# Which expert units the two one-use buffers hold: the second expert's, or the last group's first two

## The reference

```python
logits = (hf @ w_router).astype(jnp.float32) + b_router.astype(jnp.float32)
top_logit, top_e = lax.top_k(logits, TOP_K)          # 4 of 32 experts per token
gate = jax.nn.softmax(top_logit, axis=-1)
...
def expert_block(args):
    xb, e = args
    glu = xb @ w_gate[e] + b_gate[e]
    lin = xb @ w_up[e] + b_up[e]
    return clamped_swiglu(glu, lin) @ w_down[e] + b_down[e]
...
ys = lax.map(expert_block, (xs, block_e)).reshape(L, D).astype(jnp.float32) * row_gate[:, None]
out = jnp.zeros((M + 1, D), jnp.float32).at[row_tok].add(ys)[:M]
...
return rms_norm(h, final_norm_g)
```

## Time and profile before

| | |
|---|---|
| three runs, device time | 1239.42, 3041.05, 4169.03 us (median 3041.05) |
| span of the profiled execution | 1234.6 us |
| that execution's own device time | not given apart from its span; the lowest run is 4.8 us above the span |
| PE busy | 1154.9 us (94%) |
| DVE, ACT, POOL busy | 411.2, 261.5, 20.5 us |
| DMA moved | 458.40 MB, 371 GB/s over the span |
| chain that ended last | PE 64%, DMA 29%, SP's queue 3% |

### The profile page before, as it was taken

How to read it: one execution, slowest core, us unless ns; L and a number is a source line. 1 busy time by engine, 2 the same in 40 slices (tenths; PEclk the granted TensorE clock), 3 DMA queues, 4 the chain that set the end, 5 groups by cost and what they waited for, 6 DMA issues and landing times.

```text
span 1234.6 us, 16160 instructions
## 1 busy us (share of the span) xinstructions
PE 1154.9 (94%) x6694; PEld 577.1 (47%) x6694; DVE 411.2 (33%) x803; ACT 261.5 (21%) x451; POOL 20.5 (2%) x40
## 2 busy tenths in 40 slices
PE   9999999999999999999899897999988899989896
PEld 8888989887433333332233232433332333324331
DVE  5788573765421222221122112212221122122112
ACT  6556464364400010010001000100100010001001
POOL 3000000000000000000000000000000000000000
PEclk9999999999999999999999999999999999999999
DMA  7655424986799999999999999999999999999996
GB/s 285 225 200 196 180 97 186 379 319 245 273 405 416 427 421 434 431 429 434 430 435 428 433 432 429 430 429 433 431 429 434 432 432 431 429 434 431 421 415 270
DMA packets 30694, 458.40 MB, mean 371 GB/s; under 512 B 3648, under 2 KB 3664, under 8 KB 9904
## 3 DMA queue, kind: packets, MB, share of 16 engines
q1 hardware_dynamic: 29232, 454.05, 88.2%
q0 software_dynamic: 832, 2.51, 0.6%
q10 hardware_dynamic: 576, 1.07, 0.2%
HBM read 456.57 MB, written 1.05 MB: 371 GB/s over the span
## 4 chain that ended last, share of the span: by engine, by line
PE 64%; DMA 29%; SPq 3%; ACT 2%; issue 1%; DVE 1%; ACTq 0%; DVEq 0%
PE bank L1938 22%; DMA ring<-in_w_down 16%; DMA ring<-in_w_gate_up 12%; PE bank L1960 11%; PE bank L1507 5%; PE bank L1484 4%; PE sums L1594 3%; PE sums L1484 3%; PE sums L1507 3%; SPq L435 3%; PE sums L1889 3%; PE bank L1879 2%; PE bank L1594 2%; PE bank L1951 2%; PE sums L1533 1%
## 5 line engine op out<-in xcount | busy, mean ns | idle before, releaser
L1938 PE MATMUL bank<-ring,reg_a 128*64 128x512 f32 x2016 | 459.2, 607 | 39.0 <-DMA ring<-in_w_gate_up 38.2
L1938 PEld LDWEIGHTS bank<-ring,reg_a 128*64 128x64 f32 x2016 | 142.5, 139 | 322.0 <-issue 264.3
L1960 PE MATMUL bank<-ring,reg_ol 128*64 128x512 f32 x1024 | 227.2, 595 | 13.1 <-DMA ring<-in_w_down 11.6
L1401 DVE TENSOR_TENSOR masks<-bank,bT 128x256 f32<-128x256 f32 x64 | 27.2, 425 | 449.9 <-PE bank L1951 449.7
L1960 PEld LDWEIGHTS bank<-ring,reg_ol 128*64 128x64 f32 x1024 | 78.7, 137 | 140.4 <-issue 132.1
L631 ACT ACTIVATE reg_t<-bank 128x512 f32<-128x512 f32 x64 | 38.2, 597 | 440.4 <-PE bank L1938 241.7
L980 DVE SCALAR_TENSOR_TENSOR ring<-ring 128x2048 f16<-128x2048 f32 x47 | 107.4, 2290 | 46.9 <-ACT ring L649 46.7
L935 ACT ACTIVATE masks<-masks 128x256 f32<-128x256 f32 x64 | 26.7, 417 | 325.7 <-DVE masks L1402 325.7
L649 ACT ACTIVATE ring<-ring 128x2048 f16<-128x2048 f32 x47 | 89.5, 1909 | 22.9 <-PE bank L1594 6.7
L1889 PE MATMUL sums<-reg_t,reg_g 64*128 64x512 f32 x256 | 69.8, 634 | 6.2 <-ACT reg_t L631 6.2
L1388 DVE COPY reg_t<-bank 128x512 f32<-128x512 f32 x32 | 22.1, 692 | 158.8 <-PE bank L1938 158.8
(11 more groups left out here) (327 smaller groups left out, 889.1 us busy)
## 6 DMA issues: line engine op xcount, KB each, us to landing
ring<-in_w_gate_up SPq DMA_DIRECT2D x52, 4096.0 KB, 29.9
ring<-in_w_down SPq DMA_DIRECT2D x26, 4096.0 KB, 30.9
ring<-in_w_dense SPq DMA_DIRECT2D x47, 1024.0 KB, 4.9
ring<-in_w_gate_up SPq DMA_DIRECT2D x10, 2048.0 KB, 9.5
ring<-in_w_down SPq DMA_DIRECT2D x6, 2048.0 KB, 11.6
ring<-in_w_gate_up SPq DMA_DIRECT2D x24, 512.0 KB, 15.0
ring<-in_w_gate_up SPq DMA_DIRECT2D x12, 1024.0 KB, 24.5
ring<-in_w_down SPq DMA_DIRECT2D x12, 512.0 KB, 5.9
```

The costliest lines, as they stand in the source:

```text
L1938: ins = mm(pt[nh][col:col + 64, :], xg[:, c, j * SLOTS:(j + 1) * SLOTS], loaded(v + i, C, c), start=(c == 0), stop=(c == C - 1))
L1960: ins = mm(pt[2][64 * nh:64 * nh + 64, :], actT[:, 4 * i + c, :], w[:, nh * 512:(nh + 1) * 512], start=(i == 0 and c == 0), stop=(i == 1 a ...
```

## The change

`SPARE` and `EXTRA` become units 0 and 1 of the last group (`HELD = 2`). They are loaded at the same places of SP's program and into the same homes, from the last group's first expert (`held`), and PE reads them from there in the last group. The first group's units 8 and 9 go through the ring; the ring's turns of groups 0 to 6 are the unit numbers, and only the last group is shifted by two (`last_body`, `last_home`). The pieces of the first group are now those of units 8 to 13. In the last group units 2 to 11 come in pairs, units 12 to 23 in pieces as before. POOL loads the down biases and the final norm's weight once expert 0's first half of the last group is through, and PE adds the down biases ahead of expert 2 of the last group instead of ahead of expert 3 of the first. The diff:

```diff
--- before.py
+++ after.py
@@ -336,8 +336,9 @@
 
         ORDER = [(0, 0), (1, 0), (0, 1), (1, 1), (2, 0), (2, 1)]
         UPE = len(ORDER)
-        EXTRA, SPARE = NSLOT + 1, NSLOT
-        FIRST_PIECES = {10: 4, 11: 4, 12: 4, 13: 4, 14: 2, 15: 2}
+        SPARE, EXTRA = 0, 1
+        HELD = 2
+        FIRST_PIECES = {8: 4, 9: 4, 10: 4, 11: 4, 12: 2, 13: 2}
         LAST_PIECES = {UPE * (EG - 1) + i: n for i, n in enumerate((4, 4, 4, 4, 2, 4))}
         LAST_PIECES.update({UPE * (EG - 2) + i: 2 for i in range(UPE)})
         per_group = UPE * EG
@@ -354,32 +355,40 @@
             return done, already + (16 if m == 2 else 32)
 
 
-        def turn_of(v, z, first):
-
-            if z is more_rounds:
-                return v
-            return v - 2 + (first and v < EXTRA) + (first and v < SPARE)
-
-        def unit_of(turn):
-
-            return turn + 2 * (turn >= SPARE)
-
-        def home_index(v, z):
-
-            return (turn_of(v, z, False) + FIRST_SLOT) % NSLOT
+        def slot_of(turn):
+
+            return (turn + FIRST_SLOT) % NSLOT
+
+        def turn_of(v, last=False):
+
+            return v - HELD if last else v
+
+        def unit_of(turn, last=False):
+
+            return turn + HELD if last and turn >= 0 else turn
 
         def home_of(v, z, first):
 
-            if first and v == SPARE:
-                return spare, spare_ld, 0
-            w = turn_of(v, z, first)
-            s = (w + FIRST_SLOT) % NSLOT
+            s = slot_of(v)
             more = 0
             for u, n in FIRST_PIECES.items():
-                t = turn_of(u, first_round, True) if z is first_round else None
-                if t is not None and (t - w) % NSLOT == 0 and not (first and w < t):
+                if z is first_round and (u - v) % NSLOT == 0 and not (first and v < u):
                     more += 16 * (n - 1)
-            return slot[s], z.late_ld[s], 16 * (w // NSLOT + 1) + more
+            return slot[s], z.late_ld[s], 16 * (v // NSLOT + 1) + more
+
+        TURNS = per_group // NSLOT
+        LAST_PAIRS = (2, 4, 6, 8, 10)
+        LAST_WIDE = {v + i: v for v in LAST_PAIRS for i in range(2)}
+
+        def last_home(v):
+
+            s = slot_of(turn_of(v, True))
+            groups = GROUPS - 1 if s % 2 == 0 else 1
+            count = 16 * TURNS * groups + sum(16 * (n - 1) for u, n in FIRST_PIECES.items() if slot_of(u) == s)
+            for u in range(HELD, v + 1):
+                if slot_of(turn_of(u, True)) == s and u not in LAST_PIECES and LAST_WIDE.get(u, u) == u:
+                    count += 16
+            return slot[s], first_round.late_ld[s], count
 
         block = ctx.enter_context(nc.Block())
 
@@ -419,20 +428,25 @@
                     return A["w_down"][bass.ds(e, 1), :, q * WIDE + o:q * WIDE + o + n]
                 return A["w_gate_up"][bass.ds(e, 1), :, (2 * q + m) * WIDE + o:(2 * q + m) * WIDE + o + n]
 
-            def load_pair(v, e, z):
-
-                home, done, _ = home_of(v, z, False)
-                dst = ring[:, home_index(v, z) * WIDE:(home_index(v, z) + 2) * WIDE]
+            def load_pair(v, e, z, last=False):
+
+                at, (_, done, _) = (slot_of(turn_of(v, True)), last_home(v)) if last else (slot_of(v), home_of(v, z, False))
+                dst = ring[:, at * WIDE:(at + 2) * WIDE]
                 sp.dma_start(dst, columns(v, e, 0, 2 * WIDE).rearrange("e p n -> p (e n)")).then_inc(done, 16)
 
-            def load(v, e, z, first=False, piece=0, count=1):
-                home, done, _ = home_of(v, z, first)
+            def load(v, e, z, first=False, piece=0, count=1, last=False):
+                home, done, _ = last_home(v) if last else home_of(v, z, first)
                 n = WIDE // count
                 o = piece * n
                 src = columns(v, e, o, n)
-                if v in LAST_PIECES and count > 1 and not first:
+                if last and v in LAST_PIECES:
                     done, _ = piece_done(v, piece)
                 sp.dma_start(home[:, o:o + n], src.rearrange("e p n -> p (e n)")).then_inc(done, 16)
+
+            def held(v, home, o, n, done):
+
+                e = E - EG + v // UPE
+                sp.dma_start(home, columns(v, e, o, n).rearrange("e p n -> p (e n)")).then_inc(done, 16)
 
             def unit_left(v, e0, z):
 
@@ -454,21 +468,19 @@
             first = [0]
 
             def first_unit():
-                turn = first[0]
-                i = (turn + FIRST_SLOT) % NSLOT - 1
-                if turn == 0:
+                v = first[0]
+                i = slot_of(v) - 1
+                if v == 0:
                     take(sp, "pv1")
                 elif 0 <= i < EARLY:
                     dense_left(2 * i)
                     dense_left(2 * i + 1)
-                v = unit_of(turn)
                 load(v, v // UPE, first_round, True)
                 first[0] += 1
 
             def extra_half(i):
                 n = WIDE // 2
-                sp.dma_start(extra[i], columns(EXTRA, EXTRA // UPE, i * n, n).rearrange("e p n -> p (e n)"))\
-                    .then_inc(extra_ld[i], 16)
+                held(EXTRA, extra[i], i * n, n, extra_ld[i])
 
             for u, name in enumerate(HALVES):
                 if u >= EARLY:
@@ -483,7 +495,7 @@
             per = UPE * EG
             first_unit()
             take(sp, "xs3")
-            load(SPARE, SPARE // UPE, first_round, True)
+            held(SPARE, spare, 0, WIDE, spare_ld)
             take(sp, "xpv1")
             extra_half(0)
             first_unit()
@@ -504,34 +516,44 @@
                     for v in units:
                         load(v, v // UPE, first_round, True, piece, n)
 
-            reused((10, 11), 0, first_round.h_full, 1)
-            reused((12, 13), 3, first_round.h_full, 2)
-            reused((14,), 6, first_round.dn_used, 1)
-            reused((15,), 7, first_round.y_full, 1)
-            for v in range(16, per):
-                unit_left(unit_of(turn_of(v, first_round, True) - NSLOT), 0, first_round)
+            reused((8, 9), 0, first_round.h_full, 1)
+            reused((10, 11), 3, first_round.h_full, 2)
+            reused((12,), 6, first_round.dn_used, 1)
+            reused((13,), 7, first_round.y_full, 1)
+            for v in range(14, per):
+                unit_left(v - NSLOT, 0, first_round)
                 load(v, v // UPE, first_round, True)
 
-            def body(n, k, z, last=False):
-
-                def load_pieces(units):
-
-                    for v in units:
-                        unit_left(v - NSLOT, k * EG, z)
-                    for piece in range(LAST_PIECES[units[0]]):
-                        for v in units:
-                            load(v, n * EG + v // UPE, z, False, piece, LAST_PIECES[v])
-
-                for v in range(0, per - UPE if last else per, 2):
-                    if last and v in LAST_PIECES:
-                        for units in ((v, v + 1),) if ORDER[v % UPE][0] == 0 else ((v,), (v + 1,)):
-                            load_pieces(units)
-                        continue
+            def body(n, k, z):
+
+                for v in range(0, per, 2):
                     unit_left(v - NSLOT, k * EG, z)
                     unit_left(v + 1 - NSLOT, k * EG, z)
                     load_pair(v, n * EG + v // UPE, z)
-                if last:
-                    v = per - UPE
+
+            def last_body(n, z):
+
+                def slot_left(v):
+
+                    unit_left(unit_of(turn_of(v, True) - NSLOT, True), n * EG, z)
+
+                def load_pieces(units):
+
+                    for v in units:
+                        slot_left(v)
+                    for piece in range(LAST_PIECES[units[0]]):
+                        for v in units:
+                            load(v, n * EG + v // UPE, z, False, piece, LAST_PIECES[v], True)
+
+                for v in range(HELD, min(LAST_PIECES)):
+                    if v in LAST_PAIRS:
+                        slot_left(v)
+                        slot_left(v + 1)
+                        load_pair(v, n * EG + v // UPE, z, True)
+                    elif v not in LAST_WIDE:
+                        slot_left(v)
+                        load(v, n * EG + v // UPE, z, last=True)
+                for v in range(min(LAST_PIECES), per, UPE):
                     for units in ((v, v + 1), (v + 2, v + 3), (v + 4,), (v + 5,)):
                         load_pieces(units)
 
@@ -552,7 +574,7 @@
 
             with sp.Fori(ROUNDS_AT, GROUPS - 1) as n:
                 body(n, n, first_round)
-            body(GROUPS - 1, GROUPS - 1, first_round, True)
+            last_body(GROUPS - 1, first_round)
 
             for t in range(TT):
                 sp.wait_ge(fin_last, t + 1)
@@ -613,7 +635,7 @@
             root(6, 8)
             emptied(pool, "all")
             pool.tensor_scalar(over[:], st[:, 60:61], 0.0, None, ALU.is_gt).then_inc(over_ready, 1)
-            pool.wait_ge(first_round.h_full, 2 * (SPARE // UPE) + 2)
```

(34 more changed lines are left out.)

## The result

The changed kernel takes 1240.16 us (median of 20 runs, 1238.89 to 1243.68), the kernel before 1238.03 us in the same comparison. The ratio is 1.0019 with a 95% interval of 1.0012 to 1.0025: 2.1 us slower, clear of noise and far inside 2%. The lowest times of the two, 1238.89 and 1236.55 us, lie 2.3 us apart. The two runs of 3041 and 4169 us of the kernel before did not come again in its later runs and are left out of the ratio. The profiled execution of the changed kernel spans 1237.3 us against 1234.6, 2.7 us more.

What follows compares the result with a forecast made beforehand. DMA was taken to bound the expert stage, with PE setting the changed last group's end: the chain's last scatter comes 3.9 us later, span 1238.5, device time 1239.4 + 3.9 = 1243.3 us, range 1234 to 1256.

Steps and rivals of the forecast that it cites:

- the last term of the PE chain: Last group, end of expert 2's down projection to last scatter: 31.8 us less three waits, 30.4, ending at 1231.3.
- the 4.8 us put around the span: Whole execution: time outside the profiled span, lowest time 1239.42 us against span 1234.6, carried into the forecast.
- The gap: First group, 366 to 371 and 380 to 381 us: the weight stream no longer runs dry, gaining 3.8 us.
- PE's first wait for weights: Expert stage: the stream's lead over PE is gone near 490 us instead of 559.
- Start of the last group: Last group's gather: weights two places later but 3.8 us earlier, so +5.9 us, starting at 1120.8.
- Experts 0, 1, biases, expert 2: Last group's PE chain without waits: 28.0, 24.2, 3.7 and 24.2 us, ending at 1148.8, 1173.0, 1176.7 and 1200.9.
- Rival 1: Last group: DMA's last piece still sets the end, 1237.1 to 1238.5 us; chance 0.20.
- Rival 2: TensorE clock drop in the last group or late in group 6: 1251.1 us; chance 0.09.
- My 7.8 us: Price of a clock drop, from an earlier 6.16 us PE stand plus 1.67 us of slower gather matmuls.
- Rival 3: Last group: biases land late behind queued weights, if landing takes over 41 us: +53 us, about 1292 us; chance 0.03.
- Rival 4: At the end nothing changes: gap gain less the loads' cost cancels with the move, 1239.4 within 1 us; chance 0.08.

Runs made afterwards that it cites:

- e3: Kernel before with POOL's two loads issued one gate and up half later: 1238.4 us, ratio 1.0011 to the kernel before.
- e1: Changed kernel without the eight bias matmuls, POOL's loads and PE's wait for them kept: 1235.41 us, ratio 0.9987 to the kernel before.
- e2: Kernel before without the eight bias matmuls in its first group: 1235.88 us, ratio 0.9989 to the kernel before.
- f7: Changed kernel with held units, POOL's loads and bias matmuls moved from the last group to group 6: 1235.62 us, ratio 0.9985 to the kernel before.
- f8: Changed kernel with both edits of f6 and f7: 1234.82 us, ratio 0.9978 to the kernel before.
- f5: Changed kernel itself, measured again on the chip of f6, f7 and f8: 1240.09 us, ratio 1.0017 to the kernel before.
- g3: Changed kernel itself, measured again on the chip of g1 and g2: 1239.57 us, ratio 1.0015 to the kernel before.
- e4: Changed kernel with nothing held, all 24 units of the last group through the ring: 1245.87 us, ratio 1.0075 to the kernel before.
- f6: Changed kernel with down biases in homes of their own, loaded early and added in the first group: 1235.31 us, ratio 0.9983 to the kernel before.
- g1: Changed kernel with the eight bias matmuls done twice in the last group: 1248.06 us, ratio 1.0081 to the kernel before.
- g2: Changed kernel with the bias matmuls replaced by eight over all 128 rows (identity against tokens): 1239.33 us, ratio 1.0011 to the kernel before.

## Why the prediction was right or wrong

The direction and the mechanism were right; the size was too large. I forecast 3.9 us more, measured are 2.1 in the medians and 2.7 in the profiled spans. The step that failed is the last term of the PE chain, 30.4 us from the end of expert 2's down projection to the last scatter: it measured 29.2. The absolute forecast of 1243.3 us failed in a second term, the 4.8 us put around the span. The remaining 0.6 us, between 2.7 and 2.1, is a comparison of one execution of each kernel with medians. That 1240.16 us lies in the range says little: 1234 to 1256 us takes in three of the four rivals.

- **The gap.** Right. The stream behind it stands 3.8 us earlier: one pair later than the earlier trace rows would be 1105.22 + 9.72 = 1114.9, and PE's wait ended at 1111.12. e3 shows that it is not POOL's doing. PE's first wait for weights, forecast near 490 us, ended at 477.98, so the lead was gone 12 us earlier.
- **Start of the last group.** 1120.8 forecast, 1120.82 measured.
- **Experts 0, 1, biases, expert 2.** 1148.8, 1173.0, 1176.7, 1200.9 forecast; 1148.59, 1172.91, 1176.53 and 1193.86 + 7.09 = 1200.95 measured. That the biases are bare there is shown by e1, and that they were not in the first group by e2.
- **The last term was mis-sized.** From expert 2's down projection to the last scatter I took 31.8 us less the three waits of 0.63, 0.61 and 0.17: 30.4. It is 1230.17 - 1200.95 = 29.2. A wait costs more than the idle time shown: expert 3's second gate and up half took 1216.45 - 1206.71 = 9.7 us with two waits before and 1219.81 - 1211.93 = 7.9 without, so 1.24 us of idle stood for 1.86 us. Over the whole group the change adds 5.91 us at the start and 3.62 for the biases, and only 2.74 arrive at the last scatter: the waits of 5.2 us took up 6.8. The rows of the changed kernel are above; those of the kernel before are, in its PE timeline:

```profile
1206.71 3.83 PE L1938 MATMUL bank<-ring,reg_a 128*64 128x512 f32 x16
...
1213.72 1.94 PE L1938 MATMUL bank<-ring,reg_a 128*64 128x512 f32 x8 [0.61 <-DMA ring<-in_w_gate_up]
1216.45 0.66 PE L1951 MATMUL bank<-ident,reg_t 128*128 128x128 f32 x4 [0.79 <-DVE reg_t L1388]
```

  Half of the 1.2 us lies there (1.86 less 1.24), most of the rest at the down projection and its last piece.
- **The base.** I added 4.8 us to the span, from the lowest of the three runs I had. The first run of the changed kernel is 1239.89 with a span of 1237.3, 2.6 us, and the median over its 20 runs is 1.75; the kernel before has a median of 1238.03 over its 20 runs, 1.4 us under the run I took. This moved the absolute forecast, not the difference: counted from 1238.03, 1243.3 was 5.3 us more, and 2.1 were measured.
- **Rival 1** (the stream ends it) is refuted for this change: no wait for weights in the last group. In f7 and f8 the stream does end it.
- **Rival 2** (a clock drop in the bare last group) was real, but I had priced it wrongly. I argued that a group that waits less is safer. f5 and g3 show drops of 3.3 us with no wait of more than 0.21 us in the 50 us before them, at the bias matmuls that the change itself moved there. My 7.8 us were the price of another event; and a drop behind a wait, as the 8.78 us of e4, was hidden because PE still waited for weights afterwards.
- **Rival 3**: POOL's loads did land later than in the earlier trace rows, 9.2 and 20.0 us with a deep queue against 5.7 and 7.0, but far from the 41 us that would bite. The rule of the Trainium skill on turns between queue rows ("DMA: Bandwidth & Descriptors", Queues, rings and completion order) agrees with a landing within 20 us, while SP's pairs took a median of 31 us to land over the whole execution.
- **Rival 4** (no effect at the end) is excluded by the interval.
- On the clock, the Trainium skill ("TensorE: Matmul & The Clock Gate", Part 1) ties the drop to idling. These traces differ: at f5 PE's busy time is 5.00 of 5 us in each of the four stretches, and the clock still fell.

## What to carry to other kernels

In a stage that runs at the pace of a stream, PE can make up a delay only while it has slack in front of it, so what is held early was better spent a group before the end (f7) than in the last group, and extra work better put where PE is ahead (f6). Before moving work into the last group, add up the waits there: little more than that sum can be hidden. Here 5.2 us of waits hid 6.8 us of the 9.5 that were added, and 2.7 came through.

## What the runs showed of the hardware that was not expected

The granted TensorE clock fell to 1.2 GHz in an unbroken row of matmuls, in some executions, at and behind eight matmuls over 32 of the 128 rows: 3.70 us became 4.17, and 32 matmuls behind them took 9.96 us instead of 7.09 (f5; g3 alike; g1 with sixteen: 10.96 us instead of 7.3). With 128 rows, other values and the same length it did not fall in the one profile (g2). The three series of the changed kernel spread over 3.8 to 4.8 us, its variant without these matmuls over 0.8 (e1). They are not the only case: the kernel before, with them in its first group, spreads over 3.6 to 4.7 us, and over 0.95 without them (e2), while f6, f7 and f8, with them in the first group or in group 6, spread over 0.9 to 1.1. What makes the difference there is not shown.

A wait costs PE more than the idle time that the profile shows: 1.24 us of idle in two waits stood for 1.86 us.
